# The second feed-forward matrices: two products per weight tile pair in place of three

## The chip, the cores and the metric

The kernel runs on one core of a Trainium2 chip. The metric is the time of one execution on the device in microseconds (us), all the work from the first transfer to the last. A matrix product runs on TensorE (PE in the profile; its weight loads have rows of their own, PEld), elementwise work on VectorE (DVE) and ScalarE (ACT), and the queue that issues the weight transfers is SyncE's (SP).

## The reference

Two blocks of two layers each work on 256 tokens of 1024 features, in float32. Every layer has two feed-forward parts, before and after its attention part, so there are eight of them. One of them computes

```python
def swiglu(x, w_in, w_out):
    a, b = jnp.split(x @ w_in, 2, axis=-1)
    return (jax.nn.silu(a) * b) @ w_out

x = x + 0.5 * swiglu(rmsnorm(x, ffn1_norm[l]), w_ffn1_in[l], w_ffn1_out[l])
```

with `w_in` of 1024 x 5632 and `w_out` of 2816 x 1024. The change concerns the second product, `@ w_out`, alone.

## The kernel before

**Layout.** Activations lie transposed: features on the 128 partitions, the 256 tokens along the free axis. `X[:, m, :]` is feature tile m (of 8), and a product of a weight tile (128 x 128, stationary) with an activation tile (128 x 256, moving) gives 128 features by 256 tokens in one half of a PSUM bank, which has room for 512 columns. Products are numbered, product n goes to bank n modulo 8.

**Split precision.** The large products use the type `fp32r`. To keep more precision each operand is split in a high part (its value in `fp32r`) and a low part (the rest): weights in `WH` and `WL`, inputs in `UH` and `UL`, the hidden layer in `HH` and `HL`. A product is then three: high x high, low weights x high input, high weights x low input. ScalarE makes the high parts (L1520 for weights, L1524 for the input, L1537 for the hidden layer), VectorE the low parts (L1908, L1921, L1938).

**The weight feed.** SyncE's queue brings weights in slabs of at most 128 x 2048 words (1 MB) to a few places in SBUF, each when the slab before it at that place has been used up (`room`, which waits for a product's number or for `part_read`). ScalarE writes `WH` from the raw slab, then VectorE overwrites the raw slab with `WL`. `feed.to(s)` in both engines' programs says at which point of their own order slab s is split; everything behind that point in the program waits for it.

**A feed-forward part** (`ffn` in the tensor, scalar and vector programs). First 44 product tiles with `w_in` (L1070, after an opening at L1006, L1010 and L1014 which takes the input tiles one by one as they come), then the second matrix: four steps q, each with three slabs of 8, 8 and 6 hidden tiles by 256 output features. For each slab, side (0 or 1, feature tile m = 2q + side) and hidden tile k, TensorE does the three products at L1091 into columns 0 to 255 of the side's bank. After the last slab of a step side 0 is done 18 products before side 1.

**What VectorE does with the result.** `ffn` in the vector program calls `add_to_x(m)`: one instruction (L1898) that reads the bank, multiplies by 0.5 and adds X, then, once it has ended, the square of the new X tile (L1872) and its addition to a running sum (L1877), for the next norm. Then `split_low` (L1921) makes the low part of the next stage's input, after ScalarE has made the high part of the same tile (L1524, which waits for the eviction of the bank). `link` makes an instruction signal its end and VectorE wait for it. In the part called 1.1.ffn2 two more instructions a tile follow (L1887, L1889).

**What follows a part.** The part 1.0.ffn2 is followed by the opening of 1.1.ffn1, and 1.1.ffn2 by that of 2.0.ffn1. The parts 1.0.ffn1 and 1.1.ffn1 are followed by the same opening (L1006) with the mixer's first slab, 2.0.ffn1 and 2.1.ffn1 by `product_first` (L994). The parts 2.0.ffn2 and 2.1.ffn2 are followed by products that do not read X (`ple.p`, at L963). In the four `ffn1` parts the last step uses the slabs' places so that the mixer's first slabs can come in (`mixed`), and VectorE and ScalarE split slabs of the mixer (`feed.to(then)`, L1977) before the additions to X of tiles 6 and 7.

Of the kernel before, what the change touches and what calls it, by code (L numbers as in the profile page):

```python
# [31 lines left out]
P = 128  # L32
T = 256
# [4 lines left out]
FK = FF // P  # L38
# [19 lines left out]
BANKS = 8  # L58
# [396 lines left out]
def build(nc, w, vec_places, out, scratch_rows):  # L455

    pl = make_plan()
    first, slab_first = pl.first, pl.slab_first
# [6 lines left out]
    with ctx:  # L465
# [9 lines left out]
        X = sb("X", [P, DK, T])  # L475
# [50 lines left out]
        def overlay(name, shape, at, dt=FR):  # L526

            return nc.alloc_sbuf_tensor_at(name, shape, dt, offset=region_base + 4 * at)
# [5 lines left out]
            high.append(overlay(f"WH{i}", [P, SLOT], at + SLOT))  # L534


        HH, HL = overlay("HH", [P, FK, T], 0), overlay("HL", [P, FK, T], FK * T)
        OTH, OTL = overlay("OTH", [P, 4, T], 2 * DK * T), overlay("OTL", [P, 4, T], TAIL)
        MH, ML = overlay("MH", [P, DK, T], 5120), overlay("ML", [P, DK, T], 8192)
        NAH, NAL = overlay("NAH", [P, 4, T], 12336), overlay("NAL", [P, 4, T], 13360)  # L540
# [61 lines left out]
        evicted = [sem(f"evicted{b}") for b in range(BANKS)]  # L602
# [84 lines left out]
        def bank(n, *cols):  # L687
            return ps[:, n % BANKS, :] if not cols else ps[:, n % BANKS, cols[0]:cols[1]]

        def wait_product(eng, n):  # L690
            eng.wait_ge(product_done, n + 1)

        def wait_evicted(eng, n):
            eng.wait_ge(evicted[n % BANKS], n // BANKS + 1)
# [257 lines left out]
        def _(pe):  # L952
# [101 lines left out]
            def ffn(name):  # L1054
                s0, p0 = slab_first[name + ".in"], first[name + ".in"]
                u = tally.add("u", DK)
                hidden = tally.add("hidden", FK)
                for j in range(FK):
                    s = s0 + j
                    wh, wl = parts(s, DK, 256)  # L1060
                    if j == 0:
                        opening(p0, s, u)
                    else:
                        wait_split(pe, s)
                    for side in range(2 if j else 0):
                        n = p0 + 2 * j + side + 1
                        wait_room(pe, n)
                        for i, (a, b) in enumerate(((wh, UH), (wl, UH), (wh, UL))):
                            for k in range(DK):
                                last = nc.tensor.matmul(bank(n, 0, T), a[:, k, side * P:(side + 1) * P], b[:, k, :],  # L1070
                                                        start=i == 0 and k == 0, stop=i == 2 and k == DK - 1)
                        last.then_inc(product_done, 1)
                    if j == 0:
                        pe.wait_ge(constants_read, 16)
                        norm_x(first[name + ".norm"], 0)

                s = slab_first[name + ".out"]
                for q in range(DK // 2):
                    n = first[name + ".out"] + 2 * q
                    k0 = 0  # L1080
                    for t, kt in enumerate(PARTS):
                        wh, wl = parts(s, kt, 256)
                        wait_split(pe, s)
                        for side in range(2):
                            if t == 0:
                                wait_room(pe, n + side)
                            for k in range(kt):
                                if q == side == 0:
                                    pe.wait_ge(hidden_low, hidden + k0 + k + 1)
                                for a, b in ((wh, HH), (wl, HH), (wh, HL)):  # L1090
                                    last = nc.tensor.matmul(bank(n + side, 0, T), a[:, k, side * P:(side + 1) * P], b[:, k0 + k, :],  # L1091
                                                            start=k0 + k == 0 and a is wh and b is HH, stop=k0 + k == FK - 1 and b is HL)
                            if t == len(PARTS) - 1:
                                last.then_inc(product_done, 1)
                        if t < len(PARTS) - 1:
                            last.then_inc(part_read, 1)
                        k0 += kt
                        s += 1
# [118 lines left out]
            for l, L in enumerate(block1):  # L1217
# [41 lines left out]
                if l == 0:  # L1259

                    pe.wait_ge(setup_done, 1)
                    n = first["bias"]
# [588 lines left out]
        def _(dve):  # L1851
            tally = Tally()
            v_ = nc.vector

            def link(ins):

                ins.then_inc(vec_step, 1)
                dve.wait_ge(vec_step, tally.add("vec_step") + 1)
# [25 lines left out]
            def add_weighted(m):  # L1884
# [3 lines left out]
                if m:  # L1888
# [3 lines left out]
                    else:  # L1892
                        added.then_inc(squares_ready, 1)

            def add_to_x(name, factor, m):
                n = first[name] + m
                wait_product(dve, n)
                v_.scalar_tensor_tensor(X[:, m, :], bank(n, 0, T), factor, X[:, m, :], ALU.mult, ALU.add)\  # L1898
                  .then_inc(evicted[n % BANKS], 1)
                wait_evicted(dve, n)  # L1900
                add_squares(m)
# [22 lines left out]
            def ffn(name, then, gain=None, setup=None):  # L1924

                s0, p0 = slab_first[name + ".in"], first[name + ".in"]
                hidden = tally.add("hidden", FK)

                def scaled(dst, n):

                    wait_product(dve, n)
                    v_.tensor_tensor(dst, bank(n, 0, T), RSTD[:], ALU.mult).then_inc(evicted[n % BANKS], 1)

                def hidden_parts(j):

                    for i in (2 * j, 2 * j + 1):
                        dve.wait_ge(hidden_high, hidden + i + 1)
                        v_.tensor_tensor(HL[:, i, :], HF[:, i % 2, :], HH[:, i, :].bitcast(FP), ALU.subtract).then_inc(hidden_low, 1)  # L1938

                feed.to(s0 + 1)  # L1940
                for j in range(FK // 2):
                    n = p0 + 4 * j + (j > 0)
                    feed.to(s0 + 2 * j + 2)
                    if j == 0:
                        dve.wait_ge(rstd_ready, tally.add("rstd_ready") + 1)
                        norm = first[name + ".norm"]
                        if name == "2.0.ffn1":
                            v_.tensor_tensor(RSTD[:], bank(norm, T, 2 * T), V[:], ALU.mult).then_inc(evicted[norm % BANKS], 1)
                            wait_evicted(dve, norm)
                            v_.tensor_tensor(RSTD[:], RSTD[:], V[:], ALU.mult).then_inc(mean_ready, 1)  # L1950
                            dve.wait_ge(rstd_ready, tally.add("rstd_ready") + 1)
                            link(v_.tensor_tensor(RSTD[:], RSTD[:], V[:], ALU.mult))
                    elif name == "2.0.ffn1" and j <= DK:
                        link(v_.scalar_tensor_tensor(X[:, j - 1, :], X[:, j - 1, :], vec("final1", DK)[:, j - 1:j], V[:], ALU.mult, ALU.mult))
                    for side in range(2):
                        scaled(SILU[:, side, :], n + side)
                    if j > 0:
                        hidden_parts(j - 1)
                    n = p0 + 4 * j + 3
                    scaled(TMP[:, 0, 0:T], n)  # L1960
                    feed.to(s0 + 2 * j + 3)
                    scaled(TMP[:, 1, 0:T], n + 1)
                    for side in range(2):
                        i = 2 * j + side
                        wait_evicted(dve, n + side)
                        dve.wait_ge(gate_done, hidden + i + 1)
                        if i >= 2:
                            dve.wait_ge(hidden_low, hidden + i - 1)
                        v_.tensor_tensor(HF[:, side, :], SILU[:, side, :], TMP[:, side, 0:T], ALU.mult).then_inc(hidden_full, 1)  # L1969
                hidden_parts(FK // 2 - 1)  # L1970
                s = slab_first[name + ".out"]
                for q in range(DK // 2):
                    for t in range(len(PARTS)):
                        if q < DK // 2 - 1 or t == 0:
                            feed.to(s + len(PARTS) * q + t + 2)
                    if q == DK // 2 - 1 and then is not None:
                        feed.to(then)  # L1977
                    if setup is not None:
                        setup(q)
                    for m in (2 * q, 2 * q + 1):  # L1980
                        add_to_x(name + ".out", 0.5, m)
                        if gain is not None:
                            split_low(m, gain)
                        if name == "1.1.ffn2":
                            add_weighted(m)
# [631 lines left out]
```

## Time and profile before

| | |
|---|---|
| median of 3 runs | 2764.62 us (2764.57 to 2770.87) |
| the profiled execution, whole | 2762.26 us |
| its span, first to last instruction | 2760.5 us |
| mean granted TensorE clock | 0.996 |
| PE busy | 2703.6 us, 98%, 21936 products |
| DVE busy | 1837.9 us, 67% |
| ACT busy | 1301.2 us, 47% |
| chain that ended last, by line | L1070 34%, L963 32%, L1091 16% |

The span is what the profiler saw between the first and the last instruction; the execution's own time has 1.8 us around it. Products overlap in TensorE, so the duration of one (some 280 ns) is not what it adds to the time; that is the distance from the start of one to the start of the next. The chain of waits goes back from the last instruction, at each step to what released it; its pieces tell which engine set the pace in each stretch.

### The profile page before, as it was taken

The page shows a single profiled execution, that of the slowest core. Times are in us where ns is not written, and L with a number is a line of the kernel's source. Part 1 is how long each engine was busy: PE and PEld are TensorE (multiplying, and loading weights), DVE is VectorE, ACT ScalarE, POOL GpSimd, SP SyncE. Part 2 cuts the span into 40 slices and gives each one's busy share as a digit, 9 for nine tenths or more (in the row PEclk, how much of TensorE's full clock was granted, in tenths as well). Part 3 has the DMA queues.
Part 4 walks back from the last instruction along what each step waited for, and adds up shares of the span by engine and source line. Part 5 has one row for each costly group of instructions (what it writes and reads, how often), then busy time and mean ns, then how long its engine had stood idle before and what let it go on. Part 6 is the DMA issues. An engine that isn't in the chain of part 4 may idle for free.

```text
span 2760.5 us, 51012 instructions
## 1 busy us (share of the span) xinstructions
PE 2703.6 (98%) x21936; PEld 2601.8 (94%) x21936; DVE 1837.9 (67%) x3012; ACT 1301.2 (47%) x1864; POOL 71.8 (3%) x66
## 2 busy tenths in 40 slices
PE   8999999999999999999999999999999999999998
PEld 8999899999999989999999998799999999889998
DVE  5677676666666866766666657766666664676665
ACT  5445544444444555444444335444464433454443
POOL 0000100000000010000000001100000000110000
PEclk9999999999999999999999999999999999999999
DMA  7554466556555455555565753455555556444553
GB/s 264 183 168 138 138 174 201 184 180 202 184 184 156 138 168 174 177 184 179 189 205 172 208 156 116 120 173 194 185 170 192 178 184 175 130 108 164 192 187 104
DMA packets 481376, 474.68 MB, mean 172 GB/s; under 512 B 47104, under 2 KB 464512, under 8 KB 481024
## 3 DMA queue, kind: packets, MB, share of 16 engines
q1 hardware_dynamic: 477568, 460.93, 52.6%
q0 software_dynamic: 3584, 10.49, 1.4%
q8 instruction: 174, 2.85, 0.4%
q14 instruction: 50, 0.41, 0.0%
HBM read 465.09 MB, written 6.29 MB: 171 GB/s over the span
## 4 chain that ended last, share of the span: by engine, by line
PE 89%; DVE 5%; ACT 3%; DMA 1%; issue 1%; SPq 0%; DVEq 0%; ACTq 0%
PE ps L1070 34%; PE ps L963 32%; PE ps L1091 16%; PE ps L1132 2%; DVE WL L1908 1%; PE ps L1213 1%; PE ps L1177 1%; ACT WH L1520 1%; PE ps L1006 1%; PE ps L1010 1%; PE ps L1014 1%; DMA RAW<-in_w_in 1%; PE ps L1027 0%; ACT REGION L1587 0%; PE ps L994 0%
## 5 line engine op out<-in xcount | busy, mean ns | idle before, releaser
L1908 DVE TENSOR_TENSOR WL<-RAW,WH 128x2048 fp32r<-128x2048 f32 (+2 forms) x390 | 871.7, 2241 | 435.9 <-ACT WH L1520 434.2
L1520 ACT ACTIVATE WH<-RAW 128x2048 fp32r<-128x2048 f32 (+2 forms) x398 | 737.2, 1865 | 156.6 <-DMA RAW<-in_w_in 82.0
L1091 PE MATMUL ps<-HL,WH 128*128 128x256 f32 x1408 | 391.4, 278 | 0.0
L1091 PE MATMUL ps<-HH,WL 128*128 128x256 f32 x1408 | 390.8, 278 | 0.0
L1091 PE MATMUL ps<-HH,WH 128*128 128x256 f32 x1408 | 390.8, 278 | 0.0
L963 PE MATMUL ps<-UH,WH 128*128 128x256 f32 x1328 | 380.1, 286 | 2.5 <-DVE WL L1908 2.5
L1070 PE MATMUL ps<-UH,WH 128*128 128x256 f32 x2688 | 371.0, 280 | 0.8 <-DVE WL L1908 0.8
L963 PE MATMUL ps<-UL,WH 128*128 128x256 f32 x1328 | 371.7, 280 | 0.0
L963 PE MATMUL ps<-UH,WL 128*128 128x256 f32 x1328 | 371.3, 280 | 0.0
L1070 PE MATMUL ps<-UH,WL 128*128 128x256 f32 x2688 | 368.7, 280 | 0.0
L1070 PE MATMUL ps<-UL,WH 128*128 128x256 f32 x2688 | 368.7, 280 | 0.0
L1070 PEld LDWEIGHTS ps<-UH,WH 128*128 128x128 f32 x2688 | 338.0, 188 | 1.9 <-DVE WL L1908 1.0
L1070 PEld LDWEIGHTS ps<-UL,WH 128*128 128x128 f32 x2688 | 337.5, 188 | 0.0
L1070 PEld LDWEIGHTS ps<-UH,WL 128*128 128x128 f32 x2688 | 337.4, 188 | 0.0
L1091 PEld LDWEIGHTS ps<-HH,WL 128*128 128x128 f32 x1408 | 264.8, 188 | 0.0
L1091 PEld LDWEIGHTS ps<-HL,WH 128*128 128x128 f32 x1408 | 264.5, 188 | 0.0
L1091 PEld LDWEIGHTS ps<-HH,WH 128*128 128x128 f32 x1408 | 264.2, 188 | 0.0
L963 PEld LDWEIGHTS ps<-UH,WH 128*128 128x128 f32 x1328 | 250.2, 188 | 11.3 <-issue 5.6
L963 PEld LDWEIGHTS ps<-UL,WH 128*128 128x128 f32 x1328 | 250.4, 189 | 0.7 <-issue 0.5
L963 PEld LDWEIGHTS ps<-UH,WL 128*128 128x128 f32 x1328 | 250.2, 188 | 0.0
L1537 ACT ACTIVATE HH<-U 128x256 fp32r<-128x256 f32 x176 | 66.4, 420 | 272.0 <-DVE U L1969 272.0
L1524 ACT ACTIVATE UH<-X,vec_sb 128x256 fp32r<-128x256 f32 x104 | 51.4, 507 | 252.0 <-DVE X L1898 252.0
(335 smaller groups left out, 3610.2 us busy)
## 6 DMA issues: line engine op xcount, KB each, us to landing
RAW<-in_w_ffn_in SPq DMA_DIRECT2D x88, 1024.0 KB, 5.0
RAW<-in_ffn_wi SPq DMA_DIRECT2D x88, 1024.0 KB, 4.9
RAW<-in_w_in SPq DMA_DIRECT2D x86, 1024.0 KB, 5.3
RAW<-in_w_ffn_out SPq DMA_DIRECT2D x32, 1024.0 KB, 5.0
RAW<-in_ffn_wo SPq DMA_DIRECT2D x32, 1024.0 KB, 5.1
RAW<-in_w_out SPq DMA_DIRECT2D x16, 1024.0 KB, 5.2
RAW<-in_w_ffn_out SPq DMA_DIRECT2D x16, 768.0 KB, 4.4
RAW<-in_ffn_wo SPq DMA_DIRECT2D x16, 768.0 KB, 4.3
```

Source lines behind the costliest of these rows:

```text
L963: last = nc.tensor.matmul(o, a, b, start=i == 0, stop=i == len(terms) - 1)
L1006: nc.tensor.matmul(bank(n + side, 0, T), wh[:, k, side * P:(side + 1) * P], UH[:, k, :], start=k == 0, stop=False)
L1010: nc.tensor.matmul(bank(n + side, 0, T), wl[:, k, side * P:(side + 1) * P], UH[:, k, :], start=False, stop=False)
L1014: last = nc.tensor.matmul(bank(n + side, 0, T), wh[:, k, side * P:(side + 1) * P], UL[:, k, :], start=False, stop=k == DK - 1)
L1070: last = nc.tensor.matmul(bank(n, 0, T), a[:, k, side * P:(side + 1) * P], b[:, k, :], start=i == 0 and k == 0, stop=i == 2 and k == DK - 1)
L1091: last = nc.tensor.matmul(bank(n + side, 0, T), a[:, k, side * P:(side + 1) * P], b[:, k0 + k, :], start=k0 + k == 0 and a is wh and b is ...
L1132: last = nc.tensor.matmul(bank(n, 0, T), slot(s, DK, 256)[:, k, m * P:(m + 1) * P], MRG[:, k, :], start=k == 0, stop=k == DK - 1)
L1177: last = nc.tensor.transpose(dst, src, ident)
L1520: nc.scalar.activation(split_ap(s, part_high(s)), raw_ap(s), ACT.Copy).then_inc(weights_high, 1)
L1524: nc.scalar.activation(UH[:, m, :], X[:, m, :], ACT.Copy, scale=gain[:, m:m + 1]).then_inc(u_high, 1)
L1537: nc.scalar.activation(HH[:, i, :], HF[:, i % 2, :], ACT.Copy).then_inc(hidden_high, 1)
L1908: v_.tensor_tensor(split_ap(s, part_low(s)), raw_ap(s), split_ap(s, part_high(s)).bitcast(FP), ALU.subtract)\
```

## The change

The tiles `HH` and `HL` become the two halves of one tensor `HB` at the same addresses. For each hidden tile k the high weights now meet both halves in one product of 512 columns (256 tokens of the high part, 256 of the low part), which fills the whole bank; low weights x high input still goes to columns 0 to 255. The sum of the two halves of the bank is now made by VectorE, in `add_both_to_x`: one instruction more per output tile, and a `link` between the two.

```diff
-        HH, HL = overlay("HH", [P, FK, T], 0), overlay("HL", [P, FK, T], FK * T)
+        HB = overlay("HB", [P, 2, FK, T], 0)
+        HH, HL = HB[:, 0], HB[:, 1]
...
-                                for a, b in ((wh, HH), (wl, HH), (wh, HL)):
-                                    last = nc.tensor.matmul(bank(n + side, 0, T), a[:, k, side * P:(side + 1) * P], b[:, k0 + k, :],
-                                                            start=k0 + k == 0 and a is wh and b is HH, stop=k0 + k == FK - 1 and b is HL)
+                                cols = slice(side * P, (side + 1) * P)
+                                nc.tensor.matmul(bank(n + side).rearrange("p (h t) -> p h t", t=T), wh[:, k, cols], HB[:, :, k0 + k, :],
+                                                 start=k0 + k == 0, stop=False)
+                                last = nc.tensor.matmul(bank(n + side, 0, T), wl[:, k, cols], HH[:, k0 + k, :],
+                                                        start=False, stop=k0 + k == FK - 1)
...
+            def add_both_to_x(name, factor, m):
+
+                n = first[name] + m
+                wait_product(dve, n)
+                link(v_.scalar_tensor_tensor(X[:, m, :], bank(n, T, 2 * T), factor, X[:, m, :], ALU.mult, ALU.add))
+                v_.scalar_tensor_tensor(X[:, m, :], bank(n, 0, T), factor, X[:, m, :], ALU.mult, ALU.add)\
+                  .then_inc(evicted[n % BANKS], 1)
+                wait_evicted(dve, n)
+                add_squares(m)
+
...
-                        add_to_x(name + ".out", 0.5, m)
+                        add_both_to_x(name + ".out", 0.5, m)
```

## Rows read from the trace of the kernel before

**Rows 1.** The page's busy times: us, share of the span, instructions, by engine.

```profile
PE 2703.6 (98%) x21936; PEld 2601.8 (94%) x21936; DVE 1837.9 (67%) x3012; ACT 1301.2 (47%) x1864; POOL 71.8 (3%) x66
```

**Rows 2.** One of L1091's three groups: form, count, busy us, mean ns, idle before.

```profile
L1091 PE MATMUL ps<-HL,WH 128*128 128x256 f32 x1408 | 391.4, 278 | 0.0
```

**Rows 3.** Chain of waits, its L1091 pieces: start us, us, what.

```profile
138.05 36.76 PE ps L1091 x312
...
620.16 59.84 PE ps L1091 x528
...
804.09 44.90 PE ps L1091 x396
...
1287.33 62.19 PE ps L1091 x528
...
1476.75 44.90 PE ps L1091 x396
...
1956.40 59.84 PE ps L1091 x528
...
2175.24 62.20 PE ps L1091 x528
...
2657.06 59.84 PE ps L1091 x528
```

**Rows 4.** Busy time in 1.0.ffn1's stretch: length, PE, PEld, DVE, ACT, POOL, PEclk, DMA.

```profile
138.05:199.95 61.90, 61.90 (x527) 61.90 (x527) 47.60 (x77) 27.78 (x27) 0.00 (x0) 1.00 0.48 158
```

**Rows 5.** Timeline of PE, two long and two short products in turn: start us, us.

```profile
311.97 0.60 PE L1295 MATMUL ps<-REGION 128*128 128x256 f32 x2
312.40 0.39 PE L1296 MATMUL ps<-REGION 128*128 128x128 f32 x2
312.62 0.60 PE L1295 MATMUL ps<-REGION 128*128 128x256 f32 x2
```

**Rows 6.** A chain piece of L1132, and the timeline of L1051's weight loads.

```profile
470.97 13.81 PE ps L1132 x64
...
207.78 0.86 PEld L1051 LDWEIGHTS ps<-cst_sb,U 128*128 128x128 f32 x7
```

**Rows 7.** Timeline at the end of 1.0.ffn2, all engines.

```profile
678.00 0.42 DVE L1898 SCALAR_TENSOR_TENSOR X<-ps,X 128x256 f32<-128x256 f32 x1 [4.24 <-PE ps L1091]
...
679.38 0.48 DVE L1921 SCALAR_TENSOR_TENSOR UL<-X,vec_sb,UH 128x256 fp32r<-128x256 f32 x1
...
679.84 2.04 PE L1006 MATMUL ps<-UH,WH 128*128 128x256 f32 x16
680.04 0.42 DVE L1898 SCALAR_TENSOR_TENSOR X<-ps,X 128x256 f32<-128x256 f32 x1 [0.18 <-PE ps L1091]
680.50 0.51 ACT L1524 ACTIVATE UH<-X,vec_sb 128x256 fp32r<-128x256 f32 x1 [1.53 <-DVE X L1898]
```

**Rows 8.** Chain of waits at the end of 1.1.ffn1.

```profile
861.25 2.29 DVE WL L1908
863.54 0.35 DVE X L1898
...
866.24 0.50 PE ps L1006 x2
```

**Rows 9.** Chain of waits at the end of 1.1.ffn2.

```profile
1351.21 0.50 PE ps L1006 x2
```

**Rows 10.** Chain of waits at the end of 1.0.ffn1.

```profile
190.73 3.19 ACT WH L1520 x2
...
202.85 0.50 PE ps L1006 x2
```

**Rows 11.** Chain of waits at the end of 2.1.ffn1.

```profile
2238.49 5.06 PE ps L994 x41
```

**Rows 12.** Chain of waits behind 2.0.ffn2.

```profile
2016.25 6.91 PE ps L963 x32
```

**Rows 13.** The additions to X: duration ns min/median/max.

```profile
L1898 DVE SCALAR_TENSOR_TENSOR X<-ps,X x96: 404/424/425, 152.1 to 2716.9; 128x256 f32<-128x256 f32 x96
```

## The prediction

> **What bounds the kernel now.** I read the page's busy times first. TensorE is busy for 98% of the span and VectorE for 67% [rows 1], so a change can pay where TensorE's stream gets denser, and can cost where VectorE ends a wait. Then the costliest groups: each of the three products at L1091 stands there 1408 times with no idle time before it [rows 2]. 1408 is 8 parts x 8 output tiles x 22 hidden tiles; I call the three products of one of them a triple. Third, the chain of waits. Its L1091 pieces give the price of a product, length over count: 59.84 us / 528 = 113.3 ns in 1.0.ffn2, 2.0.ffn2 and 2.1.ffn2, 44.90 / 396 = 113.4 in 1.1.ffn1 and 2.0.ffn1, but 62.20 / 528 = 117.8 in 1.1.ffn2 and 2.1.ffn1 and 36.76 / 312 = 117.8 in 1.0.ffn1 [rows 3]. So there are two levels, at the same granted clock of 1.00 (2.4 GHz; rows 4 has it for a part at the upper level): a triple takes 340 ns in five parts and 353.4 in three. And three pieces are shorter than 528 products: in 1.0.ffn1 (312), 1.1.ffn1 and 2.0.ffn1 (396) the path leaves TensorE before the part is over, for the weight feed, and comes back only in the next stage. What TensorE gains behind that point is lost there.
>
> **Part 1, the products.** Columns don't change: 768 moving columns for a triple before, 512 + 256 after. What goes is one instruction and one weight load of three. Columns alone are 768 / 2.4 GHz = 320 ns, so a triple has 20 ns (lower level) or 33 ns (upper) on top, and the question is how much of it a pair keeps. The trace has no `fp32r` product of 512 columns. It has products that occupy the array as long: L1132's run at 13.81 us / 64 = 215.8 ns each, with a 128 x 128 weight load each [rows 6]. 213.3 of it would be 512 columns' time, 2.5 ns are left. A weight load by itself: seven of L1051's, whose products have one column, take 0.86 us with a last one of 0.19, so (0.86 - 0.19) / 6 = 112 ns from start to start [rows 6]. That is nearly the 113.3 of a product of 256 columns, whose own 106.7 is less. So I read the 113 to 118 as the time of a weight load that runs beside a product no longer than itself; behind a long product it costs nothing. The nearest row for the new rhythm is that of L1295 and L1296, two long and two short products in turn (the long ones with 215 ns spacing like L1132's, the short ones with about 110): from 311.97 to 312.62 us, 0.65 to 0.66 us for two long and two short, weight loads included [rows 5]. Half of it is 325 to 330 ns; I take 328 for a pair. From below a pair is bounded by 325 (216 + 109), from above by 353 (nothing gained, upper level). The two runs of 256 columns that a product now reads lie 22 KB apart; no product of the trace reads two runs, and I price that at nothing, between 0 and the 25 ns that the upper end leaves.
> The load of the next high weights still runs beside a short product, so part of the extra might stay; that is a rival below.
>
> The Trainium skill (TensorE: Matmul & The Clock Gate, Back-to-back issue gap) gives N / 2.4 + 2.5 ns for the distance of two products at full clock. For 512 columns that is 215.8, which L1132's rows agree with; for 256 it is 109.2, which the 113.3 and 117.8 of rows 3 do not. By the page alone a triple would be 327.6 and a pair 325, the change would take 2.6 ns a triple (3.2 us in all), and VectorE's cost would outweigh it: 2766.4 on the median's footing. The triple is measured, though, so of the page only the pair can hold; with 325 for it the sum would be 3.7 us better than mine.
>
> Savings per triple: 340 - 328 = 12 ns (11.9 unrounded) at the lower level, 353.4 - 328 = 25.4 at the upper one. Triples that count for the path: lower level 176 each in 1.0.ffn2, 2.0.ffn2 and 2.1.ffn2 and 132 each (396 / 3) in 1.1.ffn1 and 2.0.ffn1, together 792; upper level 104 (312 / 3) in 1.0.ffn1 and 176 each in 1.1.ffn2 and 2.1.ffn1, together 456. In 2.1.ffn1 the feed doesn't appear in the chain, since TensorE is slower there and the next slabs come early. 792 x 11.9 ns = 9.4 us, 456 x 25.4 ns = 11.6 us: 21.0 us together. The 160 triples behind the points where the path leaves bring nothing.
>
> **Part 2, VectorE's second addition.** 64 instructions of 0.42 us [rows 13] with a wait behind each; dependent instructions of this size follow at 0.46 us (680.04 to 680.50, rows 7). 29 us in all, nearly all hidden: VectorE has 14 us free of 62 even in 1.0.ffn1 [rows 4]. They show for the last tiles of a part, because the next stage's last high input tile (L1524) waits for tile 7.
> - 1.0.ffn2: TensorE goes straight to L1006, and needs tile 7's `UH` after 14 products of 0.117 us, at 680.00 + 1.64 = 681.6; it is there at 681.01 [rows 7], a reserve of 0.6. After: tile 6 keeps VectorE until 1.86 + 0.46 = 2.3 us after its start, while tile 7 is ready after 2.0; so 0.3 later, plus 0.46: 0.76. Cost 0.15 us.
> - 1.1.ffn2: two more instructions a tile, VectorE is already late, and TensorE's last two L1006 take 0.50 us for 0.23 [rows 9]. Both second additions count: 0.92.
> - 1.1.ffn1 and 2.0.ffn1: the path runs through L1908's last slab and directly into tile 6's addition, then tile 7's [rows 8]. 2 x 0.46 = 0.92 each. (Tiles 4 and 5 end before the feed's next slab.)
> - 1.0.ffn1: tiles 6 and 7, and tile 5, since ScalarE's next slab (190.73) stands behind tile 5's `UH` [rows 10]; tile 4 is hidden by a wait for ScalarE. 1.38.
> - 2.1.ffn1: TensorE already waits for tile 7 at L994 [rows 11], so the whole 0.76 counts.
> - 2.0.ffn2 and 2.1.ffn2: 6.91 us of products that don't read X follow [rows 12]. Nothing; without that cover it would be 0.76.
> Sum: 0.15 + 0.92 + 1.84 + 1.38 + 0.76 = 5.05 us.
>
> **Part 3, what moves.** Slabs are released earlier by 0.2 us a slab; the DMA share of 0.48 [rows 4] leaves room. PSUM: the number of banks is the same, only full. In 1.0.ffn1 the last six-tile slab is split 1.8 us before TensorE reads it; TensorE gains about 1.8 on it, so it comes just in time, and a wait there would lie beside the feed's path. Nothing for all of these.
>
> **Sum.** 21.0 - 5.05 = 15.9 us less: 2762.26 - 15.9 = 2746.3 for an execution like the profiled one. That one was 2.4 us under the median of 2764.62; put on the median's footing the forecast is 2748.7. One nanosecond on a pair is worth 1248 triples, 1.25 us.
>
> **The rivals.**
> - *The extra is per instruction.* The 6.6 or 11.1 ns above 106.7 stay with every product, whatever its length, and each part keeps its level. Then a pair is 333.4 or 342.3 and a triple saves 6.6 or 11.1: 792 x 6.6 + 456 x 11.1 = 10.3 us, minus 5.05: 2759.4. For it: 1.0.ffn1's level holds over all its slabs, wherever they lie. Against it: L1132's 2.5 ns.
> - *Time goes by columns at the upper level* (slower). If the two distant runs that a product now reads make every 256 columns cost 117.8, a pair is 353.4 in all parts: 792 x 13.5 = 10.7 us more, plus 5.05: 2780.3. It decides from a pair of 343 ns on in all parts. For it: three parts run at that level for no reason that the trace shows. Against it: nothing suggests a read limit, since `HH` and `HL` are read in turn already.
> - *The ends are hidden.* Pair 325 and the additions and the feed cost nothing, all 1408 triples count: 880 x 14.9 + 528 x 28.4 = 28.1 us, 2736.5. For it: the reserves in rows 7. Against it: rows 8 and 9.
> - *It doesn't do what it says*: the wide product runs as two with a weight load each. Nothing gained, 5.05 lost: 2769.7.
>
> **Chances.** The forecast with pairs of 325 to 332 ns 0.64, the per-instruction extra 0.20, columns at the upper level 0.06, ends hidden 0.07, not wide 0.03. The range of 8 in 10 goes from 2737 to 2762: below by the hidden ends, above by the per-instruction case with a few us of spread between runs. About 0.3% (8.3 us) is what a measurement of this kernel can tell from no change, so faster means under 2756.3: the first case nearly whole, the fourth, and a small share of the second, 0.74. Slower, over 2772.9: 0.06. The rest, 0.20, is the same.
>
> **What would show it.** L1091's line has two groups of 1408 products, one with 512 columns. From the start of one wide product to the next: 325 to 330 ns in all eight parts, no two levels. The second matrix then takes 57.7 us (176 x 328 ns) in a chain piece of 352 products; in the three parts of the feed the piece is shorter and L1898's successor stands behind L1908. The last two L1006 of 1.1.ffn2 start some 0.9 us later after the part's end than now. It is wrong if the pairs are at 333 or 342 (per instruction), if the piece of a part is above 60 us, or if the gaps at the openings grow by more than 1 us each.

## The result, and the profile after

The changed kernel takes 2778.21 us (median of 4 runs, 2777.46 to 2780.78). The kernel before took 2764.60 (4 runs beside it, 2763.24 to 2770.87). The ratio is 1.0052 [1.0040, 1.0064]: it is slower, by about 14 us. The forecast was 2748.7, with a range that ended at 2762; the time is next to the rival that had been given a chance of 0.06, "time goes by columns at the upper level", at 2780.3. The profiled execution took 2778.30 us with a span of 2776.5, against 2760.5 before: 16.0 us more.

Busy times of the page (engine, us, share of the span, instructions), the changed kernel:

```profile
PE 2715.2 (98%) x20528; PEld 2548.5 (92%) x20528; DVE 1864.2 (67%) x3076; ACT 1300.8 (47%) x1864; POOL 71.5 (3%) x66
```

Against [rows 1]: 1408 products and 1408 weight loads fewer, as forecast, and yet TensorE is busy for 11.6 us more. VectorE has its 64 additions, for 26 us. The costliest groups of the page, the changed kernel's second matrices (line, engine, out<-in, form, count, busy us and mean ns, idle before):

```profile
L1092 PE MATMUL ps<-HB,WH 128*128 128x512 f32 x1408 | 497.7, 396 | 0.0
L1094 PE MATMUL ps<-HB,WL 128*128 128x256 f32 x1408 | 397.0, 282 | 0.0
...
L1092 PEld LDWEIGHTS ps<-HB,WH 128*128 128x128 f32 x1408 | 264.6, 188 | 63.6
L1094 PEld LDWEIGHTS ps<-HB,WL 128*128 128x128 f32 x1408 | 264.4, 188 | 0.0
```

So the wide product is one instruction of 512 columns with one weight load, and the rival "it doesn't do what it says" is out. The remaining short product has grown longer than the three of [rows 2], 282 ns for 278. What counts is the distance from start to start. Timeline of PE in 1.0.ffn2, the changed kernel: two products that follow each other, and the wide one thirty pairs later (start us, us):

```profile
639.75 0.39 PE L1092 MATMUL ps<-HB,WH 128*128 128x512 f32 x1
639.98 0.28 PE L1094 MATMUL ps<-HB,WL 128*128 128x256 f32 x1
...
650.35 0.39 PE L1092 MATMUL ps<-HB,WH 128*128 128x512 f32 x1
```

(650.35 - 639.75) / 30 = 353.3 ns for a pair. Shared out by columns that is 235.5 for the wide product and 117.8 for the short one; the starts themselves are some 0.23 and 0.12 us apart. It isn't the clock, nor this part alone. L1092's busy time in 1.0.ffn1 and 1.0.ffn2, the changed kernel (window, length, PE busy, PEld busy, granted clock, DMA share, GB/s):

```profile
138.30:200.50 62.20, 62.08 (x176) 32.88 (x175) 1.00 0.47 157
623.70:685.84 62.14, 62.02 (x176) 32.88 (x175) 1.00 0.58 190
```

The granted clock is 1.00 (2.4 GHz) in both. From the first product to the end of the last, all eight parts now take 62.2 us; before, that held for the three at the upper level, and the five at the lower took 59.84 [rows 3]. The pair costs 353.3 ns everywhere: what a triple cost at its upper level.

**Where the 16.0 us are.** I compared, part by part, the distance from the part's first product to a product of the next stage in both traces. The level is worth 13.3 ns for the 792 triples that the prediction counted at 340 ns: 10.5 us. The ends with VectorE's second addition sum to 4.3 us. The third item was not forecast, 1.5 us after 1.0.ffn1. Together 16.3, against 16.0 in the spans; what is left is a balance of smaller differences both ways, told below.

The ends are seen best at 1.1.ffn1, in the chain of waits of the changed kernel (start us, us, what):

```profile
868.93 2.29 DVE WL L1921
871.22 0.34 DVE X L1902
...
871.59 0.43 DVE X L1903
...
873.45 0.35 DVE X L1902
...
873.82 0.44 DVE X L1903
...
874.28 0.52 ACT UH L1527
...
874.84 0.51 PE ps L1007 x2
```

Against [rows 8], the last slab is followed by tile 6's addition and then tile 7's, each now twice. From the first addition to L1007 it is 874.84 - 871.22 = 3.62 us, before 866.24 - 863.54 = 2.70: the 0.92 forecast, to the hundredth. Over the whole part, net of the level, the end costs 0.76: from the part's first product to the first of these additions the path grew by 1.59 us, where 132 triples at 13.3 ns would be 1.76.

The third item is at the end of 1.0.ffn1. TensorE reaches the last two of L1007 at 204.18, 1.33 later than in [rows 10], after 1.73 us without work (0.94 before), and the granted clock is 0.53 just after (the 1.2 GHz level for most of it). Busy time by stretch, the changed kernel (window, length, PE, PEld, DVE, ACT, POOL, granted clock, DMA share, GB/s):

```profile
203.40:204.60 1.20, 0.42 (x3) 0.42 (x4) 1.05 (x3) 0.51 (x1) 0.00 (x0) 0.94 1.09 373
204.75:208.10 3.35, 3.35 (x19) 3.35 (x18) 0.00 (x0) 0.00 (x0) 0.00 (x0) 0.53 1.08 346
208.10:212.00 3.90, 3.90 (x32) 3.80 (x32) 0.00 (x0) 0.34 (x1) 0.00 (x0) 1.00 0.17 33
```

Before, the products in that place ran at a granted clock of 1.00. Here the chain has 3.34 us for the first 16 of them and 1.88 for the next 16: 1.5 us, behind a wait that grew by 0.8 us.

Whether the change caused that fall is not shown. The same wait, 1.70 to 1.74 us, stands in this place in eleven traces (the changed kernel, e1, e2, e3, e5, e6, e7, e9, e10, e13, e17; e4, whose clock fell many times in this part, is left aside). In e2, e3, e13 and e17 the granted clock stayed at 1.00 from 204 to 208 us, in the other seven it fell. In the seven traces where the wait is 1.27 us or shorter (before, e8, e11, e12, e14, e15, e16) it did not fall here. And it fell elsewhere, in other places before and after (before, before, after; columns as above):

```profile
906.67:913.49 6.82, 5.88 (x33) 4.39 (x34) 5.78 (x13) 5.44 (x6) 0.00 (x0) 0.50 0.50 152
2050.14:2053.54 3.40, 3.40 (x17) 3.40 (x17) 3.37 (x8) 3.40 (x6) 0.00 (x0) 0.50 0.27 95
2399.24:2402.64 3.40, 3.40 (x16) 3.40 (x17) 3.40 (x5) 1.08 (x3) 0.00 (x0) 0.50 0.78 272
```

Around these three the distance between the two traces changed by -1.0, -0.9 and +1.4 us. So the 10.5 and the 4.3 us are the change's, and the 1.5 us may in part be a matter of where the clock happened to fall.

The gap of the medians (13.6) is less than 16.0. Probably that is because an execution of the kernel before isn't always like its profiled one: over all its runs it took 2754 to 2771 us, and each whole part at the upper level costs 2.35 us. The changed kernel has one level and ran from 2777.5 to 2780.8.

### The profile page after: what moved, and what is told of

It reads as the page before. It is cut to its first block, busy times and chain, and to the rows that moved or that the text cites. A ratio compares the mean times of both kernels' runs of the same rounds, so it can differ in the third digit from the quotient of the medians.

```text
span 2776.5 us, 48260 instructions
## 1 busy us (share of the span) xinstructions
PE 2715.2 (98%) x20528; PEld 2548.5 (92%) x20528; DVE 1864.2 (67%) x3076; ACT 1300.8 (47%) x1864; POOL 71.5 (3%) x66
## 4 chain that ended last, share of the span: by engine, by line
PE 89%; DVE 6%; ACT 3%; DMA 1%; issue 1%; SPq 0%; DVEq 0%; ACTq 0%
PE ps L1071 34%; PE ps L964 31%; PE ps L1092 11%; PE ps L1094 6%; PE ps L1135 2%; DVE WL L1921 1%; PE ps L1216 1%; PE ps L1180 1%; ACT WH L1523 1%; PE ps L1011 1%; PE ps L1015 1%; PE ps L1007 1%; DMA RAW<-in_w_in 1%; ACT REGION L1590 0%; PE ps L995 0%
## 5 line engine op out<-in xcount | busy, mean ns | idle before, releaser
L1092 PE MATMUL ps<-HB,WH 128*128 128x512 f32 x1408 | 497.7, 396 | 0.0
L1094 PE MATMUL ps<-HB,WL 128*128 128x256 f32 x1408 | 397.0, 282 | 0.0
L1092 PEld LDWEIGHTS ps<-HB,WH 128*128 128x128 f32 x1408 | 264.6, 188 | 63.6
L1094 PEld LDWEIGHTS ps<-HB,WL 128*128 128x128 f32 x1408 | 264.4, 188 | 0.0
L1540 ACT ACTIVATE HB<-U 128x256 fp32r<-128x256 f32 x176 | 66.4, 419 | 272.0 <-DVE U L1982 272.0
L1555 ACT ACTIVATE SILU<-SILU 128x256 f32<-128x256 f32 x176 | 65.8, 418 | 219.7 <-DVE SILU L1945 219.6
L1590 ACT ACTIVATE REGION<-REGION,MX 128x128 f32<-128x128 f32 (+3 forms) x192 | 80.1, 420 | 110.9 <-DVE MX L2084 110.6
```

Source lines behind the costliest of these rows:

```text
L1092: nc.tensor.matmul(bank(n + side).rearrange("p (h t) -> p h t", t=T), wh[:, k, cols], HB[:, :, k0 + k, :], start=k0 + k == 0, stop=False)
L1094: last = nc.tensor.matmul(bank(n + side, 0, T), wl[:, k, cols], HH[:, k0 + k, :], start=False, stop=k0 + k == FK - 1)
L1540: nc.scalar.activation(HH[:, i, :], HF[:, i % 2, :], ACT.Copy).then_inc(hidden_high, 1)
L1555: nc.scalar.activation(SILU[:, side, :], SILU[:, side, :], ACT.Silu).then_inc(gate_done, 1)
L1590: last = nc.scalar.activation(dst, src, ACT.Exp, bias=MX[:, i % 3, b, g:g + 1], scale=scale, accum_out=SUM[:, i % 3, b, g:g + 1])
```

## The experiments

Theories before the first run. A: the two distant runs of a wide product cost the 13.3 ns (the rival's own mechanism). B: the time goes by moving columns, however they are cut and wherever they lie. C: VectorE's part is right at some 5 us.

**e1 and e3, the two runs** (theory A). e1 puts the high and the low tile of one k side by side; e3 has the wide product read the high tile twice (the low tile is left out).

```diff
-        HB = overlay("HB", [P, 2, FK, T], 0)
-        HH, HL = HB[:, 0], HB[:, 1]
+        HB = overlay("HB", [P, FK, 2, T], 0)
+        HH, HL = HB[:, :, 0], HB[:, :, 1]
...
-  ... wh[:, k, cols], HB[:, :, k0 + k, :],
+  ... wh[:, k, cols], HB[:, k0 + k],
```

```diff
-  ... wh[:, k, cols], HB[:, :, k0 + k, :],
+  ... wh[:, k, cols], HH[:, k0 + k, :].unsqueeze(1).broadcast_to([P, 2, T]),
```

> The changed kernel with the two halves of HB laid side by side for each hidden tile, so that the wide product reads one run of 512 columns and not two runs 22 KB apart. Distance theory (the second run far away is what makes a wide product 235 ns): wide product 216 ns, pair about 328 ns, the second matrices 57.7 us each, time about 2749 us, faster than before. Column theory (a 4-byte moving column costs 0.46 ns in a dense stream wherever it lies, so 512 of them 235.5 ns): pair 353 ns as in the changed kernel, 2778 us. In between (340 ns): about 2765 us.

> The changed kernel whose wide product reads the high half of HB twice instead of the high and the low half; the low hidden part is left out of the product. Distance theory: the two runs are the same addresses, wide product 216 ns, pair about 328 ns. Column theory: 235 ns and 353 ns as in the changed kernel.

e1: 2778.13 us (4 runs; 2763.8 for before beside it, 13 runs), ratio 1.0054 [1.0037, 1.0071]. e3: 2776.73 (one run). The pair is unchanged in both; timeline of PE, e1, thirty pairs apart:

```profile
639.51 0.40 PE L1092 MATMUL ps<-HB,WH 128*128 128x512 f32 x1
...
650.11 0.40 PE L1092 MATMUL ps<-HB,WH 128*128 128x512 f32 x1
```

10.60 us / 30 = 353.3 ns. Theory A falls: where the second run lies, and whether there is one, costs nothing. The rival named the right price for a wrong reason.

**e2, VectorE alone** (theory C): the kernel before, its triples untouched, with its addition split in two of half the factor.

```diff
-                        add_to_x(name + ".out", 0.5, m)
+                        add_twice_to_x(name + ".out", 0.5, m)
```

> The kernel before with its three products, and only VectorE's second addition put in (each of the two takes a quarter instead of a half, from the same columns). If my costs of the stage ends hold: about 5 us over the kernel before, 2769 to 2770 us, and products at L1091 at 113.3 or 117.8 ns. If VectorE's additions carry most of the 13.6 us lost: 2775 us or more.

2767.24 us (10 runs), ratio 1.0018 [1.0005, 1.0031] to before: 3.4 us, with 5.05 inside the interval (1.4 to 8.6). The profiled run was the longest of the ten, 2774.57 us. It held a surprise, in the chain of waits of e2 (start us, us, what):

```profile
621.12 62.19 PE ps L1091 x528
...
1292.66 57.82 PE ps L1091 x510
...
1965.04 59.84 PE ps L1091 x528
```

62.19 / 528 = 117.8 ns in 1.0.ffn2, which was at 113.3 in [rows 3]; 57.82 / 510 = 113.4 in 1.1.ffn2, which was at 117.8. The levels have changed places though no product was touched, so they aren't a property of the part. This trace has 1.0.ffn1, 1.0.ffn2, 1.1.ffn1, 2.0.ffn1 and 2.1.ffn1 at the upper level. Net of that its stage ends cost 1.38, 0.28, 0.96, 1.00, 0.75, 0, 0.57 and 0 us, together 4.9.

**e4, the wide product by itself.** The product of the low weights is left out.

```diff
-                                last = nc.tensor.matmul(bank(n + side, 0, T), wl[:, k, cols], HH[:, k0 + k, :],
-                                                        start=False, stop=k0 + k == FK - 1)
```

> The changed kernel without the product of the low weights, which is left out: wide products only, each with its weight load. Column theory: 235.5 ns from wide to wide, 1408 x 235.5 ns = 332 us for the second matrices. Interplay theory (the wide product is slow because a short product and its neighbour's weight load stand beside it): 216 ns each, 304 us.

2665.29 us. Timeline of PE, e4, a run of wide products and nothing else:

```profile
629.75 11.37 PE L1092 MATMUL ps<-HB,WH 128*128 128x512 f32 x49
```

Less the 0.39 of the last one: 10.98 / 48 = 228.8 ns from wide to wide. Neither value expected came out, 216 (the price of L1132's products of the same length [rows 6]) or 235.5. So L1132's price doesn't carry over even when every second weight load is gone. The parts of this kernel are partly bound by the weight feed, with a DMA share of 0.89, so I draw no more from it.

**e5, e6, e10 and e17, where the moving tiles lie.** In the changed kernel HB moves by 24, 48, 16 and 32 words of 4 bytes, the weights stay.

```diff
-        HB = overlay("HB", [P, 2, FK, T], 0)
+        HB = overlay("HB", [P, 2, FK, T], 24)
```

> The changed kernel with HB moved up by 24 words (96 bytes), all else as it is. Address theory (the moving tiles and the weight tiles lie at certain places within a 256-byte line, and a bad pair of places makes the reads of the wide product slower): the pair leaves 353.3 ns by 5 ns or more, up or down. Column theory (a 4-byte column costs about 0.45 to 0.46 ns wherever it lies): 353.3 ns, 2778 us.

> As e5_shift_96 with 48 words (192 bytes), which puts the moving tiles at the same place within a 256-byte line as the weight tiles. Address theory: a pair other than 353.3 ns by 5 ns or more, and another one than at 96 bytes. Column theory: 353.3 ns.

> The changed kernel with HB moved up by 16 words (64 bytes); 96 and 192 bytes gave pairs of 346.7 ns, 0 bytes 353.3. If the place counts modulo 64 bytes, as a line of 16 words would make it: 353.3 ns as at 0. If it is the distance to the weight tiles' place in a 256-byte line: another value, 340 to 353.

> The changed kernel with HB up by 128 bytes. Place modulo 128 bytes: pair 353.3 ns in all parts, as at 0. Otherwise another value.

Timeline of PE, e5, thirty pairs apart:

```profile
639.81 0.39 PE L1092 MATMUL ps<-HB,WH 128*128 128x512 f32 x1
...
650.21 0.39 PE L1092 MATMUL ps<-HB,WH 128*128 128x512 f32 x1
```

10.40 / 30 = 346.7 ns, and the kernel takes 2770.59 (before: 2768.46, one run each). e6, at 192 bytes, has 346.7 as well and 2769.29; e10, at 64 bytes, 351.0 and 2776.26; e17, at 128 bytes, 353.3 and 2777.98. So half of the 13.3 ns goes when the moving tiles lie elsewhere, with the number and the length of the products unchanged. 64 and 192 bytes differ though they are 128 apart, so no simple period is shown.

**e7 and e9, the width of a column and its distance.** e7 reads only the upper two bytes of each number, of weights and of moving tiles, so its moving columns are 2 bytes wide and still 4 bytes apart. In e9 the hidden tiles are stored as two-byte numbers, and the columns are 2 bytes apart; the weights are read as in e7.

```diff
+                                def short(a):
+                                    return a.bitcast(mybir.dt.bfloat16)[..., 1::2]
+
-  ... wh[:, k, cols], HB[:, :, k0 + k, :],
+  ... short(wh[:, k, cols]), short(HB[:, :, k0 + k, :]),
```

```diff
-        HB = overlay("HB", [P, 2, FK, T], 0)
+        HB = overlay("HB", [P, 2, FK, T], 0, mybir.dt.bfloat16)
```

> The changed kernel whose second matrices read only the upper two bytes of every word of weights and hidden tiles (bfloat16 with a step of two), so that precision is left out and the number of products, columns and weight loads stays. Column theory in the form that 4-byte moving data cannot come in at 2.4 columns per ns: wide product 216 ns, short one 107 to 113, pair 323 to 330. If the extra of the wide product has nothing to do with the width of the data: 353 ns.

> As e7_two_bytes (a pair of 340.0 ns there, 226.7 + 113.3), but the hidden tiles are now written as bfloat16 side by side, so that a moving column is two bytes away from the next one and not four; low-order bits of the weights and of the hidden layer's low part are left out. Byte theory (the 17/16 cycles of a column come from reading four bytes on for every column): wide product 216 ns, pair about 325 to 330. Column theory in its hard form (a full-rate column costs 0.443 ns whatever its bytes): 340 ns again.

Timeline of PE, e7, thirty pairs apart:

```profile
639.75 0.39 PE L1095 MATMUL ps<-HB,WH 128*128 128x512 bf16 x1
...
649.95 0.39 PE L1095 MATMUL ps<-HB,WH 128*128 128x512 bf16 x1
```

The same of e9:

```profile
639.75 0.38 PE L1095 MATMUL ps<-HB,WH 128*128 128x512 bf16 x1
...
649.50 0.38 PE L1095 MATMUL ps<-HB,WH 128*128 128x512 bf16 x1
```

e7: 10.20 / 30 = 340.0 ns, 226.7 for the wide product and 113.3 for the short one; 2763.66 us. e9: 9.75 / 30 = 325.0, some 215 and 110 from start to start; 2742.62 us (before: 2765.99). Between them the moving columns move from 4 bytes apart to 2, and 15 ns a pair go. (The tiles then take half the room, so most of them start at other addresses too; but no place tried for columns 4 bytes apart gave less than 340.) The price that the forecast took for a pair, with 325 from below, holds for columns 2 bytes apart, which this kernel doesn't have. At 4 bytes the least that any run shows is 340 = 3 x 113.3 ns, the price of a triple at its lower level: against that there was nothing to save. (Both compute less precisely, so neither is a version of this kernel.) By the formula of the Trainium skill (TensorE: Matmul & The Clock Gate, Back-to-back issue gap) products of 512 and 256 columns would be an estimated 215.8 and 109.2 ns apart, 325.0 for a pair. e9's pair agrees, e7's and the changed kernel's don't; the section doesn't say how far apart its columns lie.

**e13, short weight loads**, at the old place: only 32 columns of each weight tile are loaded, and 32 rows of the output made; VectorE's two additions work on these 32 rows.

```diff
-                                cols = slice(side * P, (side + 1) * P)
+                                cols = slice(side * P, side * P + 32)
```

> The changed kernel whose second matrices load and compute only the first 32 of 128 output features of each tile (the other 96 are left out): same number of products, moving columns and weight loads, but each load reads 32 columns and not 128. Load theory (the 13.3 ns of a pair above 340 are moving reads held up by fp32r weight reads beside them): pair 340 to 344 ns. If they belong to the moving columns alone: 353.3 ns.

Timeline of PE, e13, thirty pairs apart:

```profile
639.77 0.40 PE L1092 MATMUL ps<-HB,WH 128*32 128x512 f32 x1
...
650.23 0.39 PE L1092 MATMUL ps<-HB,WH 128*32 128x512 f32 x1
```

10.46 / 30 = 348.7 ns, between the two that were expected; 2771.65 us. The load's record shrinks from 188 to 108 ns and 4.6 ns of the 13.3 go. The run makes the load and the output smaller together, so it doesn't show which of the two gives them back; that the weights' reading has a share in the extra is likely and not shown.

**e8, the order within a triple**: the kernel before with the two products of the high weights one after the other.

```diff
-                                for a, b in ((wh, HH), (wl, HH), (wh, HL)):
+                                for a, b in ((wh, HH), (wh, HL), (wl, HH)):
```

> The kernel before with the order high x high, high x low, low x high at L1091, so that the same weights come twice in a row, three products as before. If the two levels (113.3 and 117.8 ns) depend on which operands follow each other: one level in all eight parts. If they depend on how a part is entered: both levels again, in other parts than before.

2767.43 us (one run; before 2768.46). The levels are mixed again, in other parts (62.19 us / 528 in 1.0.ffn2, 1.1.ffn2 and 2.0.ffn2). This order doesn't bring one level; one trace can't say whether it shifts the odds.

**e11, e12, e14, e15 and e16, the same shifts on triples**: the kernel before with HH and HL moved by 24, 48, 8, 32 and 32 words.

```diff
-        HH, HL = overlay("HH", [P, FK, T], 0), overlay("HL", [P, FK, T], FK * T)
+        HH, HL = overlay("HH", [P, FK, T], 32), overlay("HL", [P, FK, T], FK * T + 32)
```

> The kernel before, three products, with HH and HL moved up by 24 words (96 bytes). In the changed kernel this took 6.7 ns off a pair. If the upper level of the kernel before (117.8 ns) is the clash of moving reads with weight reads at the old place: all eight parts at one level of 113.3 to 115.6 ns, and 0 to 7 us less than before (2757 to 2764 us). If the levels have nothing to do with the place: 113.3 and 117.8 in a mix again and no change in time.

> The kernel before with HH and HL moved up by 48 words (192 bytes), at the weight tiles' place in a 256-byte line. Same expectations as for 96 bytes: one level between 113.3 and 115.6 ns and 0 to 7 us less, or a mix of 113.3 and 117.8 and no change.

> The kernel before with HH and HL moved up by 8 words (32 bytes). 0 bytes gave 113.3 and 117.8 ns in a mix, 96 gave 117.3 and 118.7, 192 gave 120.0. If moving and weight reads clash by place: some value between 113.3 and 121 ns in each part, and a version that beats both kernels only if all eight are at 113.3.

> The kernel before with HH and HL moved up by 32 words (128 bytes). Same expectation as for 32 bytes; if the place counts modulo 128 bytes: 113.3 and 117.8 ns in a mix again, as at 0.

> The kernel of e15 (three products, HH and HL up by 128 bytes) timed against the kernel before. If the place counts modulo 128 bytes and the levels are a draw of each execution: same as before within 0.15%. If the place makes the lower level sure: 4 to 7 us less, 0.15 to 0.25% faster.

e11: 2776.03 us (7 runs), ratio 1.0036 [1.0024, 1.0047], 117.4 ns a product in five parts and 118.7 in three. e12: 2783.54 (4 runs), 1.0061 [1.0046, 1.0077]. A piece of its chain of waits, 1.0.ffn2:

```profile
620.14 63.35 PE ps L1091 x528
```

That is 120.0 ns, the same in all eight parts. e14, at 32 bytes, is the same (120.0; 2783.86, one run). e15, at 128 bytes, has seven parts at 113.4 and one at 117.8; 2762.62. e16 is e15's kernel again, run more often. Its chain of waits, the pieces of L1091:

```profile
138.73 35.39 PE ps L1091 x312
...
619.40 59.85 PE ps L1091 x528
...
803.32 44.91 PE ps L1091 x396
...
1285.62 57.83 PE ps L1091 x510
...
1472.75 44.91 PE ps L1091 x396
...
1953.71 59.85 PE ps L1091 x528
...
2172.82 59.87 PE ps L1091 x528
...
2653.87 59.86 PE ps L1091 x528
```

All eight are at 113.3 to 113.4 ns, where [rows 3] has three at 117.8. e16 takes 2758.20 us (9 runs, 2754.84 to 2760.02) against 2766.16 (13 runs, 2759.86 to 2769.94): 0.9970 [0.9960, 0.9980]. It beats both kernels, by two numbers in one line.

All places together, ns for the 768 moving columns of one k:

```
moved by (bytes)      0             32       64       96         128          192
triple (before)   340.0 / 353.4    360.0      -    352 / 356   340.1 (353.4)  360.0
pair (changed)       353.3           -      351.0     346.7      353.3        346.7
```

A pair was nowhere better than 346.7, and a triple is at 340 in most parts at its best place. So with numbers of 4 bytes no pair beats the best triple. At one and the same place it can: at 96 bytes the pair is 5 to 9 ns cheaper (2770.59 us in e5, 2776.03 in e11), at 192 bytes 13.3 ns (2769.29 in e6, 2783.54 in e12), VectorE's second additions included in the times. The extra above 340 thus depends on the place and on how the columns are cut, together. Of theory B the least price holds, and not its "wherever they lie".

## Why the prediction was wrong, step by step

- **What bounds the kernel**: right. TensorE's stream sets the time, the price of a product decides, and the two levels were read rightly. Wrong was to take their places for a property of the parts; e2 and e8 show them elsewhere.
- **Part 1, the products** (21.0 us saved): the step that failed. It put the 6.6 ns above 106.7 down to "the time of a weight load that runs beside a product no longer than itself; behind a long product it costs nothing". In its place: the time goes by moving columns, 0.443 ns each at the least when they are 4 bytes apart (340.0 / 768), in two products (e7) as in three (the lower level). With that least price the lower level had nothing to give, and 9.4 of the 21.0 us were never there. (By [rows 3] a triple there saves 12.0 ns and not the 11.9 of the sum, 0.1 us in all.) Of the 25.4 ns a triple of the upper level 13.4 stand above 340, which is 6.1 of the other 11.6 us; they could be had, as e16 shows, by a place at which the triples are at the lower level. The pair didn't get them: the extra of 0 to 20 ns a k depends on where the moving tiles lie and on how they are cut (e5, e6, e11, e12, e14), and at the old place the pair always pays 13.3 of it. So the upper level gave nothing, and the lower one lost 10.5.
- **Its evidence**: rows 5 and 6 are of other products. L1132's and L1295's are `f32`, in groups of two instructions of half the rate (215.8 ns for 256 columns): as long for TensorE as 512 columns, but with 256 columns read. They priced the array's time and not the reading, and the bound of 353, argued from them only as "nothing gained", was the answer. This reading of why they differ is argued; shown is that 215.8 didn't carry over (e4, e7), while columns 2 bytes apart come within 1 ns of it (e9).
- **The two distant runs** at nothing: right (e1, e3).
- **Part 2, VectorE** (5.05 us): right in kind, a little too large. Measured 4.3, in the order of the prediction 0.25, 0.91, twice 0.76, 1.09, 0.55 and nothing; e2's trace has 4.9, its timing 3.4.
- **Part 3, nothing else moves**: 1.5 us beside it. TensorE's longer wait for VectorE after 1.0.ffn1 was followed by a fall of the granted clock, in this trace and in six of the ten others with that wait. "If a gap grows, what does the clock do behind it" wasn't asked.
- **The rivals**: "columns at the upper level" met the time within 2 us with the right price, 353.4 in all parts; its reason, the two distant runs, is disproved (e1, e3), so part of that nearness is luck. Against it I had written "nothing suggests a read limit, since HH and HL are read in turn already". That argument was empty: triples, too, never went below 113.3 ns for 256 columns. "The extra is per instruction" (333 or 342) is refuted by the 353.3 of every part and by e7, where 512 columns cost twice what 256 did (226.7 and 113.3) and two products what three did.
- **The chances**: the 325 to 332 ns held 0.64 on rows that share neither type nor rate with the product in question. The trace had no such product, and the bound of 353 deserved the weight of an end that nothing excludes.

**Open**: what chooses the level of a part of triples at the old place; what the extra of 0 to 20 ns is, of which e13 takes 4.6 of 13.3 ns away and e7, with shorter loads and narrower columns at once, all 13.3; why pairs and triples pay differently at the same place; why wide products by themselves are 228.8 ns apart; whether the longer wait after 1.0.ffn1 makes the clock fall.

## What to carry to other kernels

To save instructions saves TensorE time only where the time above the columns goes by the instruction. Check the price per moving column first: if a product's start-to-start distance divided by its columns is the same at every length with the same type, merging products gives nothing, and any work that the merge puts on another engine is the result. Take a price only from products of the same type and the same distance of columns. And where the same instructions show two prices at one granted clock, try to move a tile by a few words before the loop is rewritten: here it was worth 8 us, and the rewrite cost 14. Place and cut have to be tried together: at 192 bytes the pair was the cheaper by 13.3 ns, at 0 the dearer by up to as much.

## What the runs showed of the hardware that was not expected

- Moving columns of 2 bytes cost 15 ns more per 768 when they lie 4 bytes apart than when they lie 2 apart (340.0 and 325.0, e7 and e9; the tiles' addresses differ too).
- The place of the moving tiles by itself changes the price of the same instructions from 340 to 360 ns (triples) and from 346.7 to 353.3 (pairs), at a granted clock of 1.00. The Trainium skill (SBUF — State Buffer, A bandwidth-pool intuition that's wrong) has a second read port of TensorE for the weights, which by itself would leave the moving reads alone; no run here separates the two reads, so whether the weights' reads are what disturbs the moving ones stays open.
- The same triples run at either of two prices, part by part, and not in the same parts of each kernel's trace; 128 bytes further 15 of the 16 parts of two traces (e15, e16) have the lower one.
- After a wait of TensorE of 1.70 to 1.74 us behind 1.0.ffn1 the granted clock fell in seven traces of eleven (to 0.53 over 3.35 us in the changed kernel); where the wait in the same place was 1.27 us or shorter it did not, in seven of seven.
